# Two attention stages: where the products with v stand among the transposes, and a third bank for one group

## What is computed

```python
# forgetting attention: 8 heads of 64, causal, blocks of 128 queries
s = einsum('bhqd,bhkd->bhqk', qb, kh) + Fb[..., None] - F[:, :, None, :]
p = softmax(where(kpos <= qpos, s, -inf))
o = einsum('bhqk,bhkd->bhqd', p, vh)
# differential attention: 8 heads, two score maps each, 1024 queries, 1280 keys
s = einsum('bqhzd,bkhzd->bhzqk', q, k)
p = softmax(s)
a = p[:, :, 0] - lam * p[:, :, 1]
o = einsum('bhqk,bkhe->bqhe', a, v)
```

## Time and profile before

| what | value |
|---|---|
| median of 3 runs (lowest to highest) | 2601.49 us (2599.53 to 2606.64) |
| the profiled execution, its own time | 2597.88 us |
| its span (first to last instruction) | 2596.0 us |
| mean granted TensorE clock | 0.927 of full speed |
| PE busy | 2230.3 us, 86% |
| DVE busy | 1202.3 us, 46% |
| ACT busy | 1001.6 us, 39% |

### The profile page before, as it was taken

One profiled execution on the slowest core, in us unless ns is written; L12 is line 12 of the kernel. 1 busy time (PEld: TensorE's weight loads), 2 busy tenths in 40 slices (PEclk: granted clock), 3 DMA queues, 4 the chain that ended last, 5 costly groups with the idle time before them and its releaser, 6 DMA issues. The chain is left out here.

```text
span 2596.0 us, 29037 instructions
## 1 busy us (share of the span) xinstructions
PE 2230.3 (86%) x10424; PEld 1810.8 (70%) x10424; DVE 1202.3 (46%) x1607; ACT 1001.6 (39%) x1512; POOL 606.9 (23%) x387
## 2 busy tenths in 40 slices
PE   4598488887795999999979994699999999999776
PEld 3386377776674888888868783587877777777555
DVE  3203524445414111111134647377777777776644
ACT  3512234444313111111122424256666666566521
POOL 0420022121401222222134440222221322221141
PEclk8798699998897999999989996899999999999988
DMA  2010000000223222222132421101101101100043
GB/s 95 27 48 1 18 25 25 8 24 0 82 80 115 73 73 73 73 73 73 48 121 97 156 87 49 65 25 42 37 27 47 34 32 36 44 33 29 9 166 113
DMA packets 44846, 148.14 MB, mean 57 GB/s; under 512 B 5153, under 2 KB 5809, under 8 KB 44658
## 3 DMA queue, kind: packets, MB, share of 16 engines
q1 hardware_dynamic: 38738, 125.32, 14.0%
q0 software_dynamic: 6048, 22.02, 2.4%
HBM read 130.28 MB, written 16.78 MB: 57 GB/s over the span
## 5 line engine op out<-in xcount | busy, mean ns | idle before, releaser
L207 PE MATMUL psum<-h_hi,w_hi 128*128 128x512 f32 x1072 | 427.1, 398 | 58.0 <-POOL w_lo L192 57.8
L208 PE MATMUL psum<-h_lo,w_hi 128*128 128x512 f32 x1072 | 422.8, 394 | 0.0
L209 PE MATMUL psum<-h_hi,w_lo 128*128 128x512 f32 x1072 | 422.3, 394 | 0.0
L207 PEld LDWEIGHTS psum<-h_hi,w_hi 128*128 128x128 f32 x1072 | 204.6, 191 | 103.7 <-issue 37.7
L209 PEld LDWEIGHTS psum<-h_hi,w_lo 128*128 128x128 f32 x1072 | 204.5, 191 | 43.5
L208 PEld LDWEIGHTS psum<-h_lo,w_hi 128*128 128x128 f32 x1072 | 204.7, 191 | 41.0
L1977 ACT ACTIVATE diff_probs<-psum,diff_neg_max 128x1280 f32<-128x1280 f32 x128 | 170.3, 1330 | 129.7 <-DVE diff_neg_max L2111 128.8
L2111 DVE TENSOR_REDUCE diff_neg_max<-psum 128x1 f32<-128x1280 f32 x128 | 189.5, 1487 | 55.7 <-PE psum L1680 55.5
L1364 DVE TENSOR_TENSOR hid<-psum,hid 128x512 f32 x44 | 30.4, 692 | 390.1 <-PE psum L209 390.1
L1737 PE MATMUL psum<-h_hi,w_hi 128*128 128x512 f32 x512 | 204.8, 400 | 4.3 <-ACT diff_rstd L1964 2.7
L1738 PE MATMUL psum<-h_lo,w_hi 128*128 128x512 f32 x512 | 201.8, 394 | 0.0
(11 more groups left out here) (324 smaller groups left out, 4472.2 us busy)
## 6 DMA issues: line engine op xcount, KB each, us to landing
gu_w_raw<-in_w_gu SPq DMA_DIRECT2D x44, 512.0 KB, 3.3
down_w_raw<-in_w_down SPq DMA_DIRECT2D x44, 512.0 KB, 3.2
w_whole<-in_da_w_in SPq DMA_DIRECT2D x32, 512.0 KB, 3.4
gu_ada_w<-in_ada_w SPq DMA_DIRECT2D x24, 512.0 KB, 4.2
diff_rope_half<-in_rope SPq DMA_DIRECT2D x17, 512.0 KB, 4.1
w_whole<-in_w_in SPq DMA_DIRECT2D x12, 512.0 KB, 3.4
in_y<-in_x SPq DMA_DIRECT2D x8, 512.0 KB, 6.5
gla_w_raw<-in_w_in SPq DMA_DIRECT2D x8, 512.0 KB, 3.3
```

The costliest lines, as they stand in the source:

```text
L207: pe.matmul(out, wh, rh, start=(k == 0), stop=False)
L208: pe.matmul(out, wh, rl, start=False, stop=False)
L209: last = pe.matmul(out, wl, rh, start=False, stop=(k == KT - 1))
```

## The change

Two edits.

**Differential attention.** On PE alone, in `values`, v(n) now stands in front of t(n+2) (step 0, where v(0) comes after the first units, stays as it was). Banks, buffers and waits are the same, and so are all other queues.

**Forgetting attention.** Group 1 gets a third bank, `ps[0]` (the first score bank), and a third buffer, `third`, which lies over `p_small`, the probabilities of group 0. Block kt of group 1 uses slot kt % 3, and group 0 stays on two. PE, ACT and DVE now handle blocks 0 and 1 in slot 8, block j-7 in slots 9 to 14, and none in slot 15; v(j-9) stays where it was. So t is one block further ahead of v. The waits become: t(kt) of group 1 for lo(kt-3) where kt > 2, else as before for the block two back (thus t(2) waits for lo(0)); hi likewise for v. New waits: `probs` of query block 0 for v of the group before, t(2) and t(5) for the probabilities of query block 6 (the last user of `ps[0]`), and the first score of a head for lo of the head before.

```diff
+        third_of = lambda g, kt: g == 1 and kt % 3 == 2
+        slot_of = lambda g, kt: kt % 3 if g else kt % 2
+        turn_bank = lambda g, kt: ps[0] if third_of(g, kt) else ps[4 + slot_of(g, kt)]
...
+        back = lambda g, kt: 3 if g and kt > 2 else 2
...
+        second_turns = {8: (0, 1), **{j: (j - 7,) for j in range(9, 15)}, 15: ()}
...
+                    if qb == 0:
+                        act.wait_ge(s["pv_done"], nth_pt(i, h, 0, 0) + 1)
...
-                    act.wait_ge(s["pv_done"], n + 1)
...
+                    act.wait_ge(s["pv_done"], n + 3 - back(g, kt))
...
                     if qb == 0:
+                        pe.wait_ge(s["pt_lo"], nth_pt(i, h, 0, 0) + 1)
                         pe.wait_ge(s["f_rows"], 2 * i + h + 1)
...
-                    pe.wait_ge(s["pt_lo"], n + 1)
+                    if third_of(g, kt):
+                        pe.wait_ge(s["probs"], i * UNITS + h * 8 + 9)
+                    pe.wait_ge(s["pt_lo"], n + 3 - back(g, kt))
...
                         if j >= 8:
-                            turn(i, h, 1, j - 8)
+                            for kt in second_turns[j]:
+                                turn(i, h, 1, kt)
                         if j > 8:
                             times_v(i, h, 1, j - 9)
...
                     for n in range(STEPS):
+                        if n:
+                            times_v(h, n)
                         if n + 2 < STEPS:
                             turn(h, n + 2, more)
-                        if n:
-                            times_v(h, n)
```

More of the change, by code:

```diff
@@ L775, in forgetting_attention @@
         st = ph.sb("next_qkv", [P, 3, SEQ], F32)
+        at = nc.sbuf_base
         pe_s = ph.sb("p_small", [P, 4, HALF], F32)
+        third = nc.alloc_sbuf_tensor_at("fox_pt_third", [P, 2, HALF], F32R, offset=at)
         pe_l = ph.sb("p_large", [P, 4, SEQ], F32)
@@ L794, in forgetting_attention @@
         nkt = (4, 8)
+        third_of = lambda g, kt: g == 1 and kt % 3 == 2
+        slot_of = lambda g, kt: kt % 3 if g else kt % 2
+        turn_bank = lambda g, kt: ps[0] if third_of(g, kt) else ps[4 + slot_of(g, kt)]
+        turned_hi = lambda g, kt: third[:, 0, :] if third_of(g, kt) else pt[0][:, slot_of(g, kt), :]
+        turned_lo = lambda g, kt: third[:, 1, :] if third_of(g, kt) else pt[1][:, slot_of(g, kt), :]
+        back = lambda g, kt: 3 if g and kt > 2 else 2
+        second_turns = {8: (0, 1), **{j: (j - 7,) for j in range(9, 15)}, 15: ()}
         nth_pt = lambda i, h, g, kt: i * 24 + h * 12 + g * 4 + kt
@@ L886, in turned @@
                     act.wait_ge(s["pt_turned"], n + 13)
-                    act.wait_ge(s["pv_done"], n + 1)
-                    act.activation(pt[0][:, kt % 2, c0:HALF], ps[4 + kt % 2][:, c0:HALF], ACT.Copy).then_inc(s["pt_hi"], 1)
+                    act.wait_ge(s["pv_done"], n + 3 - back(g, kt))
+                    act.activation(turned_hi(g, kt)[:, c0:HALF], turn_bank(g, kt)[:, c0:HALF], ACT.Copy)\
+                       .then_inc(s["pt_hi"], 1)
                 def body(i, more):
@@ L898, in body @@
                             piece(i + 1, slot)
-                        if j >= 4:
-                            turned(i, h, j // 8, j - 4 if j < 8 else j - 8)
+                        if 4 <= j < 8:
+                            turned(i, h, 0, j - 4)
+                        if j >= 8:
+                            for kt in second_turns[j]:
+                                turned(i, h, 1, kt)
                         if not more:
@@ L1092, in turn @@
                         pe.wait_ge(s["scaled"], i * UNITS + h * 8 + 4 * g + 6)
-                    pe.wait_ge(s["pt_lo"], n + 1)
+                    if third_of(g, kt):
+                        pe.wait_ge(s["probs"], i * UNITS + h * 8 + 9)
+                    pe.wait_ge(s["pt_lo"], n + 3 - back(g, kt))
                     for b in range(max(kt - 4 * g, 0), 4):
-                        last = pe.transpose(ps[4 + kt % 2][:, b * P:(b + 1) * P],
+                        last = pe.transpose(turn_bank(g, kt)[:, b * P:(b + 1) * P],
                                             block_of(4 * g + b)[:, kt * P:(kt + 1) * P], core.ident[:, :])
@@ L1104, in times_v @@
                     pe.wait_ge(s["pt_lo"], n + 3)
[L1105 to L1108, removed]
+                    out = ps[O_BANK][:, c0:HALF]
+                    hi, lo = turned_hi(g, kt)[:, c0:HALF], turned_lo(g, kt)[:, c0:HALF]
+                    pe.matmul(out, v[0][:, kt, :], hi, start=(kt == 0), stop=False)
+                    pe.matmul(out, v[0][:, kt, :], lo, start=False, stop=False)
+                    pe.matmul(out, v[1][:, kt, :], hi, start=False, stop=(kt == nkt[g] - 1))\
                       .then_inc(s["pv_done"], 1)
```

4 lines of the change are left out of this document (2 added, 2 removed).

## The result

The changed kernel takes **2617.04 us** (median of 16 runs, 2605.89 to 2621.39) against 2601.95 us before (16 runs, 2596.69 to 2606.70): ratio 1.005, 95% interval [1.004, 1.006]. It is slower, by 15 us, where the prediction said 10. That is the upper edge of the forecast's own +5 to +15, and 2617 lies in the range of 2596 to 2622. The profiled execution is one of the long ones: 2621.39 us, span 2619.5, where the median is 2617.04.

The account below looks back on a forecast made before the run. PE, busy 86% of the span, bounds the kernel, so only its waits count. Seven heads +10.9, last head +3.7, forgetting attention -4.6: +10.0 us, forecast 2611 us; own range +5 to +15, full range 2596 to 2622.

Parts of the forecast that it names:

- The sign and the mechanism: Differential attention: slower, as t(n) to its v(n) needs 2.00 us and the new order leaves 1.48.
- The squares' wait: Differential attention, heads with units: PE's wait before the squares grows from 0.96 to 1.74 us.
- v(17)'s: Differential attention, end of a head with units: v(17) waits about 0.6 us.
- v(19)'s: Differential attention, end of a head with units: wait grows from 1.87 to about 2.1 us.
- A head with units, 1.56: Differential attention: each of seven heads 1.56 us longer, 10.9 us in all; bounds nothing and 22.
- The two delays: Heads with units: squares 0.78 us later through t(10), and t(15) another 0.78 later behind them.
- Rival 1: Clock falls more often: a 1.6 us spell in each of seven heads, +11, so 2622 us; chance 0.16.
- The chain from t(10): Heads with units: t(10) 0.78 us later, through hi(10) and ACT's square, delays the squares with no slack.
- The last head, 3.7: Differential attention, head without units: 2.1 us over 8 steps, 0.78 at v(16), 0.78 at t(18); bounds 1.5 and 6.
- Forgetting attention, -4.6: Gain of 2.4 us in three pairs with units and 2.2 in the last pair; bounds 1 and 8.
- Rival 2: Slack absorbs the delays of t: differential attention unchanged, forgetting attention's gain stays, 2597 us; chance 0.20.
- rival 3: Differential attention: products in front end the 19.4 us of waits at the first product of v, 2577 us; chance 0.12.

Follow-up runs that it names:

- wait_filled: Changed kernel plus eight unread 512-column matmuls between v(18) and v(19) in the seven heads with units; 2606.74 us, ratio 1.0027.

## Why the prediction was right, and where it was short

- *The sign and the mechanism were right.* One block of lead fewer for t makes ACT's copy late, and PE pays at waits further on. The squares' wait was forecast at 1.74 (1.65) and v(17)'s at 0.6 (0.41). v(19)'s was forecast to grow to 2.1 and didn't (1.85).
- *A head with units, 1.56: short.* The two delays gave 0.70 and 0.69, 1.39 together, a bit under forecast. What made the head 2.9 longer is 1.5 of clock. This is the mis-sized term of the sum: 10.9 us forecast for seven heads, 20 measured in the trace.
- *Rival 1, the clock, happened, and I gave it 0.16.* Its fall was priced well (1.6; measured 1.5), and its 2622 is the forecast's 2611 with seven of them on top; the measured 2617 lies halfway between the two, and the range held it because its upper end was laid at this rival. My argument against it was that six of seven waits of 1.87 had passed. That treated the wait's length as what decides. It stayed at 1.85 and the fall went from one head in seven to seven. The chance ought to have been near that of the forecast, and cases with some falls belonged between the two.
- *The chain from t(10)* was followed as if each link began when the last one ended. That was true of the links, but t(11) enters this queue too: with t(10) put back 0.47 of the 0.70 remained. The step read the chain that ended last and not the one just under it.
- *The last head, 3.7:* 4.3, in part by luck. Two steps take 2.8 us where 2.78 was forecast, with a wait of v in about every second one and not in nearly every one, and v(16) waits 3.03 for its chain instead of 2.46, 0.57 more where 0.78 was forecast. But from v(16) to v(19), where the prediction had 0.78 for one more v in front of t(18), it took 1.4 us more, at a mean clock of 0.52 against 0.63; how much of that is the order isn't shown. In the profiles of the kernels with this order in all steps the last head takes 35.6 to 37.5 us. Start of v(6) and of v(8):

```profile
2463.62 0.50 PE L2304 MATMUL psum<-diff_pt_hi,diff_v_hi 128*128 128x512 f32 x1 [1.02 <-DVE diff_pt_lo L2160]
...
2466.43 0.50 PE L2304 MATMUL psum<-diff_pt_third,diff_v_hi 128*128 128x512 f32 x1 [0.28 <-DVE diff_pt_third L2160]
```

- *Forgetting attention, -4.6:* -6.05 by the traces, -4.0 by the medians of the edit alone. In the traces the pairs with units give 2.9 us (2.4 forecast) and the last pair 3.2 (2.2 forecast). Group 1 starts as forecast, the wait of 1.05 moved from v(0) to t(2):

```profile
396.36 0.66 PE L1120 MATMUL psum<-ident,fox_p_large 128*128 128x128 f32 x4 [1.05 <-DVE fox_pt_lo L1014]
396.77 0.47 PE L1132 MATMUL psum<-fox_pt_hi,fox_v_hi 128*128 128x512 f32 x1
```

- *The sum with what was measured:* 7 x 1.39 + 4.3 - 6.05 = +8.0, close to the +10.0, with terms that were off both ways; `wait_filled`, which has exactly this and no fall behind v(19), measured +7.0. With seven falls of 1.5 it is +18.5, and the kernel before has falls too, one to two in the profiles of its order. That gives 15 to 17, and +15 was measured. That single executions differ in the number of falls fits the scatter of the changed kernel (two runs of 16 at 2606, most at 2613 to 2621); it is argued from there and not shown, as one execution alone was profiled, and `wait_filled`, whose profile has no such fall, scatters from 2603.54 to 2610.87 too.
- *Rival 2* (delays absorbed) and *rival 3* (waits of v gone) did not occur: the waits at v grew.

## What to carry to other kernels

Where products on one engine need a result that goes round through two others, count the work that lies between a block's request and its use against the length of that round trip (here 2.00 us against 1.48); the loss shows up at whatever hangs on those engines' queues later, and a handful of steps can carry all of it. Before calling a delayed chain settled, look for the second chain that enters the same queue just behind it. And when a change lengthens or shifts waits of PE of a microsecond or two, give the clock a case of its own *on top of* the waits, with a fair chance even if most such waits passed before: a loop that gets longer meets the clock's falls at other places. Then try filling the wait that the fall follows, even by half.

## What the runs showed of the hardware

I had not expected that one wait of 1.85 us, the same in both kernels, would cost 1.5 us more in seven heads of seven after it had in one of seven. The clock's record in the traces shows what goes with it, for waits of this length. In the changed kernel (us):

```
start of v(19)       1786.68  1888.94  1991.24  2093.51  2195.81  2298.17  2400.37
start of the spell   1787.42  1889.82  1992.22  2094.62  2197.02  2299.42  2401.82
```

```profile
1786.92:1787.42 0.50, 0.50 (x3) 0.38 (x3) 0.30 (x1) 0.00 (x0) 0.00 (x0) 1.00 0.00 0
1787.42:1787.92 0.50, 0.50 (x4) 0.40 (x2) 0.00 (x0) 0.16 (x1) 0.00 (x0) 0.50 0.00 0
```

The spells start 102.40 us apart each time, while the v(19) are 102.20 to 102.36 apart: the spells keep a beat of their own. In each of the thirteen traces the starts of all spells (31 to 40) lie on one even beat, to 0.005 us. Nine traces have the wait of v(19) unfilled, 63 places in all. Where the next beat, counted on from the spells, comes 0.05 to 1.46 us after v(19) starts, the clock fell in 35 places of 35; where it comes 1.60 to 2.92 us after, in none of 26; in two places a beat lay just ahead of v(19), and one fell (0.22 us ahead) and one didn't (0.11 us ahead). Shorter waits before it, of the squares (0.9 to 1.65) and v(17), don't change that. In the kernel before, a head of 99.4 us shifts v(19) against the beat each time, and one of seven was hit; the changed head, 102.3 us long with its fall, comes back to nearly the same place, and all seven were. So seven of seven was partly chance: it hangs on the length of the head.

With the wait filled, by products or by transposes, or half filled, so that 0.93 is left, the clock stays at its upper level behind v(19) in all seven heads, though by that count four of the seven (three with transposes) stood where an unfilled wait fell. So the filling did not help by a shift in time alone. On the Trainium skill's rule on transposes, quoted with that run, the measurement decides: transposes held the clock here.
